# mLSTM denominators as columns: a 128x4 reciprocal, spread back over the partitions by products with the identity

## The reference

```python
def mlstm_chunked(q, k, v, logi, logf, C0, n0, m0):
    ...
    def step(carry, xs):
        C, n, m = carry
        q_c, k_c, v_c, b_c, d_c, dmax_c, s_c = xs
        m_t = jnp.maximum(b_c + m[..., None], dmax_c)
        w_inter = jnp.exp(b_c + m[..., None] - m_t)
        w_intra = jnp.exp(d_c - m_t[..., None])
        a = s_c * w_intra
        num = w_inter[..., None] * jnp.einsum('bhtk,bhkv->bhtv', q_c, C) + jnp.einsum('bhts,bhsv->bhtv', a, v_c)
        den = w_inter * jnp.einsum('bhtk,bhk->bht', q_c, n) + jnp.sum(a, axis=-1)
        h = num / jnp.maximum(jnp.abs(den), jnp.exp(-m_t))[..., None]
        ...
```

## Time and profile before

| | us |
|---|---|
| median of 3 runs | 2608.99 |
| the runs | 2608.93 to 2610.06 |
| the profiled execution, device time | 2611.51 |
| its span, first to last instruction | 2609.8 |
| TensorE busy in the span | 2564.2 (98%) |
| VectorE busy | 2105.4 (81%) |
| ScalarE busy | 1213.3 (46%) |
| mean granted TensorE clock | 0.995 of full |

### The profile page before, as it was taken

One profiled execution on the slowest core, in us unless ns is written; L12 is line 12 of the kernel. 1 busy time (PEld: TensorE's weight loads), 2 busy tenths in 40 slices (PEclk: granted clock), 3 DMA queues, 4 the chain that ended last, 5 costly groups with the idle time before them and its releaser, 6 DMA issues.

```text
span 2609.8 us, 43704 instructions
## 1 busy us (share of the span) xinstructions
PE 2564.2 (98%) x17600; PEld 2533.9 (97%) x17600; DVE 2105.4 (81%) x2614; ACT 1213.3 (46%) x1921; POOL 355.2 (14%) x186
## 2 busy tenths in 40 slices
PE   9999999998999999999999999999999999999998
PEld 9999999998999799999999999999999999999998
DVE  7979786887787889898877998988757788898756
ACT  5535454343444545455445554645311355454445
POOL 2200003332010120000024200000333300000042
PEclk9999999999999999999999999999999999999999
DMA  4223323232114423223323222223322222332231
GB/s 127 82 81 92 87 78 90 61 84 78 53 36 111 130 65 90 82 82 91 88 71 94 71 83 81 82 85 91 88 77 74 61 78 81 90 89 82 84 97 49
DMA packets 420251, 215.13 MB, mean 82 GB/s; under 512 B 19218, under 2 KB 418011, under 8 KB 420048
## 3 DMA queue, kind: packets, MB, share of 16 engines
q1 hardware_dynamic: 406066, 205.36, 27.6%
q10 hardware_dynamic: 13982, 6.96, 1.0%
HBM read 204.58 MB, written 7.68 MB: 81 GB/s over the span
## 4 chain that ended last, share of the span: by engine, by line
PE 56%; DVE 8%; ACT 2%; issue 1%; POOL 0%; DVEq 0%; ACTq 0%
PE ps L1124 13%; PE ps L1126 13%; PE ps L1125 13%; PE ps L1109 5%; PE ps L1110 5%; PE ps L1113 5%; PE ps L1182 1%; PE ps L1184 1%; PE ps L1183 1%; DVE sumsq L2666 1%; DVE ut L2561 1%; DVE x L3389 1%; DVE tau_lo L2630 1%; DVE r L2752 0%; DVE x L3574 0%
## 5 line engine op out<-in xcount | busy, mean ns | idle before, releaser
L1057 POOL TENSOR_TENSOR wlo<-raw,whi 128x1024 fp32r<-128x1024 f32 (+2 forms) x150 | 339.7, 2266 | 2215.9 <-ACT whi L1852 2215.9
L1124 PE MATMUL ps<-tau_hi,whi 128*128 128x320 f32 x1280 | 396.2, 309 | 0.5 <-ACT sq L2090 0.5
L1125 PE MATMUL ps<-tau_lo,whi 128*128 128x320 f32 x1280 | 395.9, 309 | 0.0
L1126 PE MATMUL ps<-tau_hi,wlo 128*128 128x320 f32 x1280 | 395.9, 309 | 0.0
L1863 ACT CAST whi<-raw 128x512 fp32r<-128x512 f32 (+4 forms) x368 | 258.1, 714 | 195.3 <-PE ps L1126 189.3
L1109 PE MATMUL ps<-xh,whi 128*128 128x320 f32 x1040 | 317.0, 313 | 4.2 <-POOL wlo L1057 2.3
L1110 PE MATMUL ps<-xl,whi 128*128 128x320 f32 x1040 | 313.4, 309 | 0.0
L2577 DVE TENSOR_TENSOR wlo<-raw,whi 128x512 fp32r<-128x512 f32 (+4 forms) x368 | 289.4, 801 | 17.3 <-ACT whi L1863 17.1
L1109 PE MATMUL ps<-hh,whi 128*128 128x320 f32 x928 | 282.4, 312 | 4.4 <-DVE hl L3018 2.1
L1110 PE MATMUL ps<-hl,whi 128*128 128x320 f32 x928 | 280.3, 310 | 0.0
L2577 DVE TENSOR_TENSOR wlo<-wsum,whi 128x1536 fp32r<-128x1536 f32 (+2 forms) x112 | 180.8, 1614 | 81.8 <-ACT whi L1863 80.3
(11 more groups left out here) (498 smaller groups left out, 6120.0 us busy)
## 6 DMA issues: line engine op xcount, KB each, us to landing
raw<-in_ffn_w_gu SPq DMA_DIRECT2D x320, 256.0 KB, 3.8
raw<-in_ffn_w_d SPq DMA_DIRECT2D x96, 192.0 KB, 3.0
raw<-in_w_in_even SPq DMA_DIRECT2D x32, 512.0 KB, 4.1
raw<-in_ffn_w_d SPq DMA_DIRECT2D x32, 384.0 KB, 3.6
raw<-in_w_in_odd SPq DMA_DIRECT2D x24, 512.0 KB, 3.8
raw<-in_ffn_w_gu SPq DMA_DIRECT2D x16, 512.0 KB, 4.3
raw<-in_ffn_w_d SPq DMA_DIRECT2D x64, 128.0 KB, 2.7
raw<-in_w_ple_gate SPq DMA_DIRECT2D x16, 512.0 KB, 4.1
```

The source lines that it names most:

```text
L1057: pool.tensor_tensor(ring(wlo, n), raw[:, slot, 0:kt, :], ring(whi, n).bitcast(fp32), ALU.subtract).then_inc(lo_ready, 1)
L1124: pe.matmul(out, whi[:, w], hi(i), start=(start and i == 0), stop=False, skip_group_check=True)
L1125: pe.matmul(out, whi[:, w], lo(i), start=False, stop=False, skip_group_check=True)
L1126: last = pe.matmul(out, wlo[:, w], hi(i), start=False, stop=(i == kt - 1), skip_group_check=True)
```

## The change

The denominators are made with the tokens in the partitions: one column of 128 numbers for each head. The weights (a, or q) become the stationary operand, and the column of ones, or the normaliser's column, the moving one. Absolute value, maximum and reciprocal then work on 128x4. Four products with the identity (part `rden`) spread each column of reciprocals over the partitions again, into bank 2 (prompt) or 6 (sample), and ScalarE copies the 128x512 result to SBUF. The floor is taken as columns, too: the transposed gate rows are in bank 7 anyway (part `kin`; in the sample tile one transpose takes the place of an unused one), so the floor's rows, their store and their five loads go.

```diff
-        gate_rows = nc.dram_tensor("gate_rows", (6, 4, T), fp32, kind="Internal").ap()
-        ROWS = "beta G gates qin floor kend".split()
+        gate_rows = nc.dram_tensor("gate_rows", (5, 4, T), fp32, kind="Internal").ap()
+        ROWS = "beta G gates qin kend".split()
...
+        fcol = sb("fcol", [P, 4])
+        dcol = sb("dcol", [P, 4])
...
-        ML_PE = "qk vt kin kt num den up0 up1".split()
-        ML_ACT = "gates qin floor vt kin kt den".split()
-        ML_DVE = "qk q out up0 up1".split()
+        ML_PE = "qk vt kin kt num den up0 rden up1".split()
+        ML_ACT = "gates qin vt kin kt den rden".split()
+        ML_DVE = "qk q rden out up0 up1".split()
...
                 pe.wait_ge(core["xr"], half_at(t, L - 1, 1))
                 per_head(3, lambda h: pS[:, h], lambda h: W(0)[:, h]).then_inc(core["ks"], 1)
+                mlstm_part(t, "rden")
                 z_fill(s, filled, Z_KS)
...
                 pe.wait_ge(core["utok"], t + 1)
+
+                pe.wait_ge(ml_act, ml(ML_ACT, t, "rden"))
                 for h in range(HA):
...
                 pe.wait_ge(ml_dve, ml(ML_DVE, t - 1, "up1"))
-                unused_products(bank(6)[:, 0:P], 6)
+                sample_part("floor")
+                unused_products(bank(6)[:, 0:P], 5)
...
                 sample_part("den")
                 state_c(1)
+                sample_part("rden")
                 sample_part("nsum")
...
+                elif part == "floor":
+                    last = pe.transpose(bank(7)[:, 0:P], R2[:, tile(t)], ident[:])
...
-                        pe.matmul(bank(6)[:, hs:hs + P], one[:].to_broadcast([P, P]), VS(3)[:, h], start=True, stop=False)
-                        last = pe.matmul(bank(6)[:, hs:hs + P], one[:].to_broadcast([P, P]), VS(7)[:, h], start=False, stop=True)
+                        pe.matmul(bank(6)[:, h:h + 1], VS(3)[:, h], one[:], start=True, stop=False)
+                        last = pe.matmul(bank(6)[:, h:h + 1], VS(7)[:, h], one[:], start=False, stop=True)
+                elif part == "rden":
+
+                    pe.wait_ge(ms_dve, MS_DVE.index("rden") + 1)
+                    last = per_head(6, lambda h: dcol[:, h:h + 1].to_broadcast([P, P]), lambda h: ident[:])
...
-                        pe.matmul(bank(6)[:, h * P:(h + 1) * P], one[:].to_broadcast([P, P]), V(3)[:, h], start=True, stop=False)
-                        last = pe.matmul(bank(6)[:, h * P:(h + 1) * P], pC[:, h, P:MW].to_broadcast([P, P]), q[:, h],
-                                         start=False, stop=True)
+                        pe.matmul(bank(6)[:, h:h + 1], V(3)[:, h], one[:], start=True, stop=False)
+                        last = pe.matmul(bank(6)[:, h:h + 1], q[:, h], pC[:, h, P:MW], start=False, stop=True)
+                elif part == "rden":
+
+                    pe.wait_ge(ml_dve, ml(ML_DVE, t, "rden"))
+                    last = per_head(2, lambda h: dcol[:, h:h + 1].to_broadcast([P, P]), lambda h: ident[:])
...
                 elif part == "kin":
+                    act.activation(fcol[:], bank(7)[:, 64:64 + HB], ACT.Exp)
                     last = act.activation(kcol[:, 0:4], bank(7)[:, 96:96 + HB], ACT.Exp)
...
+                elif part == "den":
+                    last = act.activation(dcol[:], bank(6)[:, 0:HB], ACT.Abs)
                 else:
-                    last = act.activation(V(7), heads(6), ACT.Abs)
+                    last = act.copy(V(7), heads(2))
...
-                            for part in {2: ["gates", "qin"], 3: ["floor", "vt", "kin"], 4: ["kt"], 6: ["den"]}.get(l, []):
+                            for part in {2: ["gates", "qin"], 3: ["vt", "kin"], 4: ["kt"], 6: ["den"]}.get(l, []):
...
-                                if t:
-
-                                    act.wait_ge(ml_dve, ml(ML_DVE, t - 1, "out"))
-                                    load_floor(t)
...
                         z_copy(4 * t + 2)
+                        mlstm_part(t, "rden")
 
                         act.wait_ge(core["rt"], t + 1)
...
                     act.wait_ge(ms_pe, MS_PE.index("den") + 1)
-                    act.activation(VS(0), heads(6), ACT.Abs).then_inc(ms_act, 1)
+                    act.activation(dcol[:], bank(6)[:, 0:HB], ACT.Abs).then_inc(ms_act, 1)
                     prep(z0 + 9)
+
+                    act.wait_ge(ms_pe, MS_PE.index("rden") + 1)
+                    act.copy(VS(0), heads(6)).then_inc(ms_act, 1)
...
+                mlstm_part(t, "rden")
 
                 dve.wait_ge(core["ks"], t + 1)
                 own(dve.tensor_tensor(W(6), v, heads(3), ALU.subtract).then_inc(core["rT"], 1), core["rT"])
                 if t < NTILE - 2:
                     beta_products(t + 1)
-                mlstm_part(t, "scale")
...
                 dve.wait_ge(ms_act, MS_ACT.index("den") + 1)
-                o1(dve.tensor_tensor(VS(0), VS(0), VS(2), ALU.max))
-                o1(dve.reciprocal(VS(0), VS(0)))
+                o1(dve.tensor_tensor(dcol[:], dcol[:], fcol[:], ALU.max))
+                ms(dve.reciprocal(dcol[:], dcol[:]))
+
+                dve.wait_ge(ms_act, MS_ACT.index("rden") + 1)
...
-                elif part == "scale":
+                elif part == "rden":
 
                     dve.wait_ge(ml_act, ml(ML_ACT, t, "den"))
-                    o1(dve.tensor_tensor(V(7), V(7), V(2), ALU.max))
-                    o1(dve.reciprocal(V(7), V(7)))
+                    o1(dve.tensor_tensor(dcol[:], dcol[:], fcol[:], ALU.max))
+                    own(dve.reciprocal(dcol[:], dcol[:]).then_inc(ml_dve, 1), ml_dve)
                 elif part == "out":
+
+                    dve.wait_ge(ml_act, ml(ML_ACT, t, "rden"))
                     own(dve.tensor_tensor(v, heads(7), V(7), ALU.mult).then_inc(ml_dve, 1), ml_dve)
```

More of the change, by code:

```diff
@@ L373, in stream_step @@
         qin_loaded = sem("qin_loaded")
-        floor_loaded = sem("floor_loaded")
         kend_loaded = sem("kend_loaded")
@@ L419, in stream_step @@
         ml_pe, ml_act, ml_dve = sem("ml_pe"), sem("ml_act"), sem("ml_dve")
-        ML_PE = "qk vt kin kt num den up0 up1".split()
-        ML_ACT = "gates qin floor vt kin kt den".split()
-        ML_DVE = "qk q out up0 up1".split()
+        ML_PE = "qk vt kin kt num den up0 rden up1".split()
+        ML_ACT = "gates qin vt kin kt den rden".split()
+        ML_DVE = "qk q rden out up0 up1".split()
         ms_pe, ms_act, ms_dve = sem("ms_pe"), sem("ms_act"), sem("ms_dve")
-        MS_PE = "qk vt kt den nsum".split()
-        MS_ACT = "gates qin floor kend vt kt den".split()
-        MS_DVE = "qk q nq kend n out".split()
+        MS_PE = "floor qk vt kt den rden nsum".split()
+        MS_ACT = "floor gates qin kend vt kt den rden".split()
+        MS_DVE = "qk q nq kend rden n out".split()
         def ml(steps, t, name):
@@ L1483, in sample_tile @@
                         sample_part("qk")
+                        pe.wait_ge(ms_act, MS_ACT.index("floor") + 1)
                         unused_products(bank(7)[:, 0:P], 2)
@@ L1637, in sample_part @@
                     for h in range(HB):
-                        hs = h * P
-                        pe.matmul(bank(6)[:, hs:hs + P], one[:].to_broadcast([P, P]), VS(3)[:, h], start=True, stop=False)
-                        last = pe.matmul(bank(6)[:, hs:hs + P], one[:].to_broadcast([P, P]), VS(7)[:, h], start=False, stop=True)
+                        pe.matmul(bank(6)[:, h:h + 1], VS(3)[:, h], one[:], start=True, stop=False)
[3 more added lines that the diff above has]
+                    last = per_head(6, lambda h: dcol[:, h:h + 1].to_broadcast([P, P]), lambda h: ident[:])
                 else:
@@ L2013, in mlstm_part @@
                     last = act.activation(V_in(t), V_in(t), ACT.Exp)
-                elif part == "floor":
-                    act.wait_ge(floor_loaded, 16 * (t + 1))
-                    last = act.activation(V(2), V(2), ACT.Exp)
                 else:
                     act.wait_ge(ml_pe, ml(ML_PE, t, part))
-                if part in ("gates", "qin", "floor"):
+                if part in ("gates", "qin"):
                     pass
                 elif part == "kin":
+                    act.activation(fcol[:], bank(7)[:, 64:64 + HB], ACT.Exp)
                     last = act.activation(kcol[:, 0:4], bank(7)[:, 96:96 + HB], ACT.Exp)
@@ L2291, in _ @@
                             act.wait_ge(rows_ready, 1)
-                            for name, rows, first in (("beta", R1, 0), ("G", R1, 32), ("gates", R2, 0), ("qin", R2, 32), ("floor", R2, 64), ("kend", R2, 96)):
+                            for name, rows, first in (("beta", R1, 0), ("G", R1, 32), ("gates", R2, 0), ("qin", R2, 32), ("kend", R2, 96)):
                                 act.dma_start(gate_rows[ROWS.index(name)], rows[first:first + 4, :]).then_inc(rows_stored, 16)
@@ L2319, in load_gates @@
                         act.dma_start(V_in(t), row_at("qin", t)).then_inc(qin_loaded, 16)
-                    def load_floor(t):
```

(7 more changed lines are left out.)

## The result

| | before | after |
|---|---|---|
| median of 14 runs each, us | 2612.02 (2608.19 to 2616.28) | 2617.52 (2612.71 to 2619.77) |
| mean of the runs, us | 2611.82 | 2616.97 |
| profiled execution (span), us | 2611.51 (2609.8) | 2617.81 (2616.1) |
| VectorE busy, us | 2105.4 | 2086.6 |
| mean granted clock, profiled execution | 0.995 | 0.994 |

The changed kernel takes 1.002 times the time of before, 95% interval 1.0013 to 1.0028: slower by 0.2%, clear of the noise. The prediction said 2612.8 and no change that can be told. Its range ended at 2617.0, half a microsecond short.

A forecast was written before the change was run, and what follows sets the result against it. TensorE's work was taken as the path, not VectorE's reciprocal. Four tile ends at 0.88 plus 0.27 in the sample tile gave 3.8 us on 2608.99, so 2612.8, no change that can be told; range 2608.0 to 2617.0.

The forecast's parts named there:

- The mechanism at the prompt tiles: Prompt tile ends: TensorE's work is the path, so added `rden` delays the chain and VectorE's savings become idle time.
- The reciprocal off the path: Prompt tile ends: VectorE's 3.35 us reciprocal is done 0.24 us before the longer chain, so removing it gains nothing beyond.
- Rival (c): Tile ends: VectorE is the path after all, nearly 4 us each come off, total 2593; chance 0.05.
- rival (a): Denominators: one-column products are cheap, at most 4.0 us off in all and sample `rden` hidden, total 2608.5; chance 0.09.
- `rden` 0.88 at each tile end: Four prompt tile ends: eight added TensorE instructions between `ks` and the fillers delay the chain 0.88 us, bounds 0.8 to 1.0.
- the idle 0.56 gives nothing back: Prompt tiles: TensorE's 0.56 us wait for `utok` lies inside the same chain, so it recovers none of `rden`'s cost.
- I cost them at nothing: ScalarE's edits, including six removed small DMA issues, count zero because its waits for TensorE in the levels, 58.9 us, cover them.
- The sample tile 0.27: Sample tile: `rden` adds 0.88 us, 0.61 of idle time goes, so `state_s(0)` starts 0.27 later.
- small reciprocal: Sample tile: it moves behind the square root, is through at 871.5, before the addition waiting for TensorE, and costs nothing.
- rival (b): One-column products drop TensorE's clock, likeliest in the sample tile; 1.7 us per fall, 2614.5 to 2621.3; chance 0.17.
- The base: The sum was put on the runs' median, 2608.99 us, not the profiled 2611.51, as the difference does not touch the terms.

The follow-up runs named there:

- e4: Changed kernel with the prompt tiles' `rden` moved from before the fillers into TensorE's wait for `utok`; 2614.00 us, ratio 1.0010 to before.
- e5: Changed kernel with 128 equal columns moving instead of one in the sample tile's sixteen denominator products; 2616.08 us, ratio 1.0012 to before.
- e3: Changed kernel with eight more unread transposes between the sample tile's one-column products; 2618.97 us, ratio 1.0027 to before.
- e9: Kernel before with only the sample tile changed, 128 equal columns moving in its denominator products instead of one; 2613.10 us, ratio 1.0001.
- e11: Sample tile alone changed, with 128 columns moving in its denominators, plus ScalarE's cast of the projection's weights moved earlier; 2610.94 us, ratio 1.0001 to before.
- e1: Kernel before with the change in the four prompt tiles alone, old sample tile kept; 2614.19 us, ratio 1.0013 to before.
- a8: The changed kernel itself, unaltered, run again beside the follow-up kernels; 2617.04 us, ratio 1.0015 to before.
- e10: Kernel before plus 22 unread products at the core's start and full products replacing the sample tile's unread transposes; 2610.16 us, ratio 0.9994.

## Why the prediction was wrong

The mechanism at the prompt tiles held. Three steps of the sum failed: it stood on the median of three runs, which was 3 us too low; in the sample tile it had 0.27 us where the traces show 0.9, since it left out the queue behind the square root; and it put the clock at nothing, where the runs show about 4 us more at the lower level, worth 1.6 to 2.0. Two gains of 0.53 and 0.34 that it did not foresee cover part of this.

**The reciprocal off the path: right.** VectorE is busy for 18.8 us less and idle time stands in their place; no prompt tile is shorter by it. Rival (c) is refuted in every tile.

**One-column products, rival (a): refuted.** Sixteen take 1.71 us at the upper clock, 0.107 each. The spacing of some 25 ns that the Trainium skill names on its page "TensorE: Matmul & The Clock Gate", section "Back-to-back issue gap", is that of isolated products; none of the runs shows it where each product has its own weight load.

**`rden` 0.88 at each tile end: right,** 0.89 measured. That the idle 0.56 gives nothing back was right for the place it was put in, yet moved into it `rden` costs 0.08 (e4).

**"I cost them at nothing", of ScalarE's removed DMA issues: wrong once, in the good direction.** The cover was looked for in the levels, but the floor's first load stands ahead of them. GpSimd and VectorE at the core's start, before and then after:

```profile
637.64 2.34 POOL L1057 TENSOR_TENSOR wlo<-raw,whi 128x1024 fp32r<-128x1024 f32 x1 [6.63 <-ACT whi L1852]
639.05 1.61 DVE L2760 SCALAR_TENSOR_TENSOR qkv<-qkv,inv 128x640 f32<-128x640 f32 x1
```
```profile
637.11 2.35 POOL L1058 TENSOR_TENSOR wlo<-raw,whi 128x1024 fp32r<-128x1024 f32 x1 [6.07 <-ACT whi L1868]
639.07 1.06 DVE L2770 SCALAR_TENSOR_TENSOR qkv<-qkv,inv 128x640 f32<-128x640 f32 x1
```

The issue of 0.53 stood ahead of ScalarE's cast, the cast ahead of GpSimd's subtraction, and VectorE's product again ends 0.67 behind that. The first `decays` starts at 640.4 to 640.6 in all eight traces with new prompt tiles and at 641.0 to 641.3 in the six with old ones. Another 0.34 went from the period 43.18, which became 43.72 like the others: a wait before VectorE's first instruction of that tile was longer in the old kernels, and why stays open. So the prompt part is 4 x 0.89 - 0.53 - 0.34 = 2.7 us, not 3.5. Traces with the same fall of 10.2 us at the core's start agree: the sample tile's `decays` starts at 818.1 and 818.2 with new prompt tiles (e5, e3) and at 815.2 to 815.7 with old ones (before, e9, e11). e1's mean lies 3.2 above before, with an interval of 1 to 5.5.

**The sample tile 0.27, with the small reciprocal "costs nothing": the mechanism fell.** The forecast followed the reciprocal, and it was indeed in time for the addition. It did not follow the rest of ScalarE's queue behind the square root, to the cast and to GpSimd, which is never named in it. That made 0.2 into 0.9 at the end of the first normalisation (e9), and moving the cast gave 1.31 back (e11), more than was lost, since this product is held up in before as well, 1.55 instead of 0.89.

**The clock, rival (b): true, in one place.** It was given 0.17 and its likeliest place named, the sample tile behind other narrow products. All five profiles with one-column products there have a fall at them, three at their end and two, those of the changed kernel and a8, from 1 to 2 us ahead of them on, and none has one in a prompt tile behind the core's start; the mistake was to count as unlikely what the rows of before had already shown once for narrow products. The size of 1.7 us for a fall was about right: the runs of the changed kernel have 4 us more at the lower clock than those of before (2617 x 2 x (1 - 0.9942) = 30, against 26 at before's 0.9950), and run by run, in before and in the changed kernel, a microsecond at that level goes with 0.4 to 0.5 us of time, so 1.6 to 2.0. The 4 us have an uncertainty of about 1.5; the wide kernels, whose clocks lie near that of before, put most of it on the narrow shape.

**The base: wrong by 3 us.** The sum was put on the median of three runs, 2608.99, and the profiled 2611.51 was set aside because a difference of 2.5 "does not touch" the terms. It touches the time: the median of 14 runs is 2612.02, near the profile. Of the 4.7 us by which the predicted time was missed, 3.0 are this and 1.7 the terms above. The forecast ratio, 2612.8 / 2608.99 = 1.0015, lies inside the measured interval. That is in part luck: 0.9 us of gains that were not foreseen stand against some 2.4 of losses that were not.

Together 2.7 + 0.9 + 1.6 to 2.0 is 5.2 to 5.6, against 5.15 between the means. The parts of the sample tile are only known to some tenths, that of the clock to about a microsecond.

## What to carry over

When an instruction moves, follow the queue behind it to its last user, other engines included: here a square root 0.9 us later reached VectorE by way of a cast and GpSimd. A reciprocal that overlaps a longer chain is worth nothing, and what replaces it must lie in that chain's waits (e4), not ahead of them. Base a forecast on as many runs as there are, and where three runs and the profile differ, keep both in the range.

## What the runs showed of the hardware

VectorE's product of two SBUF tensors does not finish while GpSimd's subtraction of 128x1024 runs: 2.20 us instead of 0.89 when it starts 0.83 behind it, and always ended 0.67 to 0.69 behind its end. The addition with one operand in PSUM, beside the same subtraction, took its usual 1.41 for two. The Trainium skill, page "SBUF — State Buffer", section "SBUF: two separate sides", says that the two engines share a pair of ports that one of them holds for a whole instruction, against VectorE operations with two SBUF inputs among others; the traces agree.

The granted clock fell at the end of sixteen fp32 products of one column in three of three profiles where it had been full before them, also with eight transposes in between (e3), and in none of seven with 128 columns moving and the same weights. Where it had just fallen ahead of these products it came back after 10.2 us with one column (the changed kernel, a8) and after 3.4 with 128 (e9, e10); but elsewhere in the same tile falls of 3.4 and of 10.2 us come without such a difference. A reciprocal of 128x4 took 0.18 us and one of 128x512 3.35.
